# Head 4's root ahead of a pool operand, statistics two k steps sooner at four entries, and the first four low parts on VectorE

## What is computed

```python
h = rms_norm(x, g[0])                 # x0, x2: entries of the two mixers
m = parallel_conv_mla(h, ...)         # or conformer_conv
x = x + rms_norm(m, g[1])
h = rms_norm(x, g[2])                 # x1, x3: entries of the two MLPs
x = x + rms_norm(squared_relu_mlp(h, mlp_w1[i], mlp_w2[i]), g[3])
...
n1 = _rmsnorm(h, norm1_w)             # x4: entry of the second block
q, k, v, fg, u = jnp.split(n1 @ w_in, [...], axis=-1)
q = _rmsnorm(q.reshape(B, L, N_HEADS, HEAD_DIM), q_norm_w)
k = _rmsnorm(k.reshape(B, L, N_HEADS, HEAD_DIM), k_norm_w)
pooled = [_trailing_mean_minus_self(u[group g], w) for g, w in enumerate((2, 4, 8, 16))]
```

## Time and profile before

| | us |
|---|---|
| three runs | 1783.16, 1784.21, 1779.24; median 1783.16 |
| the profiled execution, its own time | 1780.72 |
| its span, first to last instruction | 1778.9 |
| TensorE busy | 1742.8, 98% |
| GpSimd busy | 886.8, 50% |
| VectorE busy | 793.2, 45% |
| ScalarE busy | 662.8, 37% |

### The profile page before, as it was taken

One profiled execution on the slowest core, in us unless ns is written; L12 is line 12 of the kernel. 1 busy time (PEld: TensorE's weight loads), 2 busy tenths in 40 slices (PEclk: granted clock), 3 DMA queues, 4 the chain that ended last, 5 costly groups with the idle time before them and its releaser, 6 DMA issues.

```text
span 1778.9 us, 22989 instructions
## 1 busy us (share of the span) xinstructions
PE 1742.8 (98%) x8243; PEld 1448.7 (81%) x8243; DVE 793.2 (45%) x1221; ACT 662.8 (37%) x1039; POOL 886.8 (50%) x477
## 2 busy tenths in 40 slices
PE   8999999999999999999999999999899999999999
PEld 6887887888888877878788888889878888888887
DVE  7458654301331479956430132147757244444200
ACT  6338543312222446554321232145357332222221
POOL 5457545444444469755544444445345644444442
PEclk9999999999999999999999999999999999999999
DMA  5532123233333213122333333322210333323332
GB/s 179 130 105 60 36 71 103 91 102 95 95 97 100 76 48 107 59 86 92 106 95 95 96 100 99 95 71 72 86 49 10 98 95 94 94 95 97 104 106 71
DMA packets 46074, 158.45 MB, mean 89 GB/s; under 512 B 5745, under 2 KB 6001, under 8 KB 46001
## 3 DMA queue, kind: packets, MB, share of 16 engines
q1 hardware_dynamic: 46000, 157.45, 28.5%
HBM read 153.10 MB, written 2.10 MB: 87 GB/s over the span
## 4 chain that ended last, share of the span: by engine, by line
PE 88%; DVE 6%; ACT 3%; issue 2%; POOL 1%; DMA 1%; SPq 0%; DVEq 0%; POOLq 0%; ACTq 0%
PE PS L1830 26%; PE PS L1832 25%; PE PS L1831 25%; PE PS L1899 2%; DVE PS L1218 1%; PE PS L1935 1%; PE PS L1930 1%; PE PS L1931 1%; PE PS L2091 1%; DMA raw<-weights 1%; DVE PS L1210 1%; PE PS L1840 0%; DVE XLR L1218 0%; ACT wh L727 0%; PE PS L2114 0%
## 5 line engine op out<-in xcount | busy, mean ns | idle before, releaser
L548 POOL TENSOR_TENSOR wl<-raw,wh 128x1024 fp32r<-128x1024 f32 x220 | 533.0, 2424 | 632.1 <-ACT wh L741 198.3
L1831 PE MATMUL PS<-XLR,wh 128*128 128x512 f32 x1216 | 474.4, 390 | 0.0
L1830 PE MATMUL PS<-XHR,wh 128*128 128x512 f32 x888 | 349.0, 393 | 9.3 <-POOL wl L617 6.0
L1832 PE MATMUL PS<-XHR,wl 128*128 128x512 f32 x888 | 346.8, 391 | 0.0
L1831 PEld LDWEIGHTS PS<-XLR,wh 128*128 128x128 f32 x1216 | 229.2, 188 | 47.3
L1830 PE MATMUL PS<-HH,wh 128*128 128x512 f32 x688 | 267.6, 389 | 0.0
L1831 PE MATMUL PS<-HL,wh 128*128 128x512 f32 x688 | 267.6, 389 | 0.0
L1832 PE MATMUL PS<-HH,wl 128*128 128x512 f32 x688 | 267.6, 389 | 0.0
L727 ACT ACTIVATE wh<-raw 128x1024 fp32r<-128x1024 f32 x123 | 128.6, 1055 | 240.0 <-PE PS L1832 196.6
L1830 PEld LDWEIGHTS PS<-XHR,wh 128*128 128x128 f32 x888 | 167.6, 189 | 45.1 <-POOL wl L617 6.4
L1832 PEld LDWEIGHTS PS<-XHR,wl 128*128 128x128 f32 x888 | 167.4, 189 | 35.1
(11 more groups left out here) (343 smaller groups left out, 2577.9 us busy)
## 6 DMA issues: line engine op xcount, KB each, us to landing
raw<-weights SPq DMA_DIRECT2D x287, 512.0 KB, 3.5
X<-x_t SPq DMA_DIRECT2D x8, 256.0 KB, 6.8
out_t<-X SPq DMA_DIRECT2D x8, 256.0 KB, 4.6
KH<-rope_h SPq DMA_DIRECT2D x4, 128.0 KB, 4.6
KL<-rope_l SPq DMA_DIRECT2D x4, 128.0 KB, 5.4
QH<-XHR SPq DMA_DIRECT2D x16, 32.0 KB, 2.0
QL<-XLR SPq DMA_DIRECT2D x16, 32.0 KB, 2.0
pos_i<-positions SPq DMA_DIRECT2D x1, 256.0 KB, 8.3
```

The lines of the kernel that those rows point to most:

```text
L548: pool.tensor_tensor(wl[:, j], raw[:, j], wh[:, j].bitcast(F32), ALU.subtract).then_inc(w_lo, 1)
L1830: pe.matmul(out, wa, xa, start=start, stop=False)
L1831: pe.matmul(out, wa, xb, start=False, stop=False)
L1832: return pe.matmul(out, wb, xa, start=False, stop=stop)
```

## The change

It has three parts. VectorE makes `wl` of blocks 0 to 3, one after each even x tile, and GpSimd waits for all four before its first block (4). In `enter_residual` the statistic stands at k = 3 in place of 5 and the spread at 5 in place of 7, at x1, x2, x3 and x4. On ScalarE `head_root(4)` stands directly behind `head_square(4)`, ahead of `pool_operand(3)` and `hi(n0 + 13)`.

```diff
-            lo_range(0, 5)
+            pool.wait_ge(w_lo, RING)
+            lo_range(RING, 5)
             zero_rows((KH, KL), 5, 0)
...
             head_square(4)
+            head_root(4)
             pool_operand(3)
             hi(n0 + 13)
-            head_root(4)
             head_round(4)
             head_square(5)
...
             for k in range(KT):
                 v.wait_ge(xh, k + 1)
                 stt(XL[:, k], X[:, k], ENTRY_GAIN["x0"](k), f(XH[:, k]), ALU.mult, ALU.subtract).then_inc(xl, 1)
+                if k % 2 == 0:
+                    v.wait_ge(w_hi, k // 2 + 1)
+                    tt(wl[:, k // 2], raw[:, k // 2], f(wh[:, k // 2]), ALU.subtract).then_inc(w_lo, 1)
...
-                tile(n0 + 3, last, {5: lambda: stat(entry), 7: lambda: spread(entry)},
+                tile(n0 + 3, last, {3: lambda: stat(entry), 5: lambda: spread(entry)},
                      order=range(ahead, KT), begun=True)
```

## The result

The changed kernel took 1766.18 us, median of 5 runs (1765.94 to 1770.06), against 1780.31 for the kernel before, median of 5 (1779.24 to 1784.21). The ratio is 0.9919, with a 95% interval from 0.9908 to 0.993: 14.1 us less. The profiled execution took 1765.98 us, 14.7 less than that of before. The forecast was 1772 us, in a range from 1766 to 1779, and the prediction's parts made 9.7.

A forecast was written before the change was run, and what follows sets the result against it. TensorE, busy 98% of the span, was taken as the bound. Parts 2.0 + 4.5 + 3.2 = 9.7 us gave 1771.0 from the profiled 1780.7 or 1773.5 from the median 1783.2; forecast 1772, range 1766 to 1779.

The forecast's parts named there:

- Part 1: Start: `wl` of four blocks on VectorE lets low parts of x come sooner; 2.0 us, between -0.8 and 2.3.
- Both terms: Start: TensorE goes on 0.9 us sooner after the fourth low part of x; two later waits going give 1.1.
- The two waits: Behind the start: TensorE's waits for `rcol` (0.3) and the latents' `ssq` (0.8) both go, 1.1 us.
- The loss of 1.7 by clock: Start: one more 3.5 us stretch at half clock would cost 1.7 us, making the low bound -0.8.
- Part 2: x1 to x4: statistics two k steps sooner; x1 and x3 2.7 together, x2 1.4, x4 0.4, sum 4.5 us.
- the wait named: x2: TensorE's wait of 5.97 us, until 670.64, becomes 1.36 shorter, down to 4.6.
- Rival (d): x entries: the statistics do nothing, as TensorE meets the block's `wl` instead of the bank; about 1777, chance 0.06.
- Part 3: Head 4: root sooner, so the wait ahead of its spread shrinks by 2.8 to 3.8; 3.2 us taken.
- the sentence on the clock behind the spread: Head 4: a shorter wait may leave the clock up from 1262.50 to 1266.50, saving 1.7; only in the high bound, 5.5.
- Rival (a): Head 4: its wait moves on to head 5, part 3 gives 1.5 or less; about 1778, chance 0.13.
- Rival (b): Head 4 and x2: no low-clock stretch after head 4, a shorter one at x2; 13 us, about 1768, chance 0.14.
- Rival (c): Start: clock stays at 1.2 GHz through the first four tiles; loss 21.8 less 9.7, time 1795, chance 0.02.

The follow-up runs named there:

- the filled start: Kernel before, with 8 matmuls that compute nothing needed in TensorE's start wait of 2.36 us for the second low part of x: 1780.71 against 1781.3, ratio 0.9996.
- the last experiment: Changed kernel with spread at k = 4 and filling matmuls in the layer norm's pairs, ahead of its spread and in head 4's last wait: 1768.48, ratio 0.9919.
- The filled wait: Kernel before, with 12 matmuls that compute nothing needed in TensorE's 3.8 us wait ahead of head 4's spread: 1775.95 against 1780.36, ratio 0.9977.
- GpSimd's load: Changed kernel with four GpSimd subtractions of a `wl`'s size, which nothing reads, put back at the start: 1772.57, ratio 0.9959.

## Why the prediction was wrong, step by step

**Part 1, 2.0 forecast, 3.1 measured.** The mechanism and the durations were right (`wl` on VectorE 1.22 against 1.26, low parts 0.74 against 0.74). Both terms were too small, by 0.6 and 0.4. TensorE went on at 12.69, not at 13.0, and the rest of the serial list was sooner too: 1.49 at the statistic of x0 where 0.9 stood. The two waits gave 1.46 where 1.1 stood. The loss of 1.7 by clock, the low bound, concerns a stretch that costs nothing in the kernel before (the filled start) and comes and goes; it does cost where TensorE has work through it, 2.2 us in the last experiment. The Trainium skill, "TensorE: Matmul & The Clock Gate", What's actually happening, says that the moment of a change is not tied to the kernel's start. The traces agree for the start and attention: two profiles of one kernel differ there.

**Part 2, 4.5 forecast, 4.4 measured.** x1 1.29 and x3 1.34 for 1.36 each, x2 1.37 for 1.4, x4 0.39 for 0.4. At x2 the size was right but not the wait named, so that the size came out is in part luck: the wait of 5.97 became 5.79 and not 4.6, and most of the rest was a wait of 0.92 for ScalarE's `wh` ahead of it, which I had not listed and which is gone. Rival (d) fell.

**Part 3, 3.2 forecast, 7.1 measured: the step that failed.** The wait shrank by 2.95, within the 2.8 to 3.8 given and for the reason given: `meta_x` was held up behind `pool_l`, 1.17 us for 0.21. The Trainium skill, "GPSIMD Engine Reference", Key points, made no exception for small copies, and the trace agrees with that. What failed is the sentence on the clock behind the spread, worth 1.7 "where VectorE isn't the one to wait for". I left it out of the sum and allowed it once. It was worth 4.1. The stretch that I had priced at 1.7 gave 2.15, and a second one behind head 5, which I had not counted, 1.97. VectorE was waiting for TensorE's products, so the low clock lay on the path twice, in TensorE's own list and in VectorE's, where small instructions slipped behind GpSimd. The filled wait gives the same 4.1 as the shortened one, so this is clock and not wait; only the second stretch's tie to the wait stays open. Rival (a) fell. Rival (b) was the right one in kind for head 4, with too small a price; the stretch at x2, its other half, did not get shorter.

**Outside the parts.** Attention gave 1.54 in the profile. That is not the change's: the stretch there is absent from the second profile of the kernel before too. Between x2 and x3 1.30 were lost, by the layer norm's longer stretch, which differs between two profiles of the kernel before as well (774 to 778 and 773.5 to 779.5). That the two nearly cancel, and so that the parts come close to the whole, is luck. 9.7 + 1.1 (part 1) - 0.1 (part 2) + 3.9 (part 3) + 1.5 - 1.3 = 14.8. The forecast of 1772 lay 1 us above the sum from the profiled execution, since it allowed for a median of 1783.2; with two more runs the median of the kernel before was 1780.31.

**Rival (c)** fell. Its condition, low clock while TensorE has work at the start, was seen in the last experiment and cost 2.2, a tenth of its price, as the clock was back by 18 us. Under GpSimd's load it cost 1.5.

What stays open: what decides whether a low stretch of the start, the layer norm or attention appears, and for how long. Runs of one kernel differ by 4 to 5 us, about as much as such stretches cost. The mean granted clock of each run points the same way: of the changed kernel's ten runs the five from 1765.9 to 1766.2 us have 0.996, the five from 1767.1 to 1770.1 have 0.994. By an estimate from these shares, 0.002 of 1764 us is 3.5 us of clock lost, or some 7 us more at half clock. Where in those longer runs the stretches lay, no profile shows.

## What to carry to other kernels

A long wait of TensorE is worth its own length and then the low clock behind it, if the engines that follow wait for TensorE's products there; count every low stretch behind it, and what slips behind another engine's long instructions meanwhile. A low stretch that ends inside a wait is worth nothing. That other engines are busy throughout is no proof that it is worth nothing. To price it, fill the wait with spare matmuls: here that held the clock and left the wait's end where it was. Fill one wait at a time, and read the gain from marks right behind it, or one filling's loss hides another's gain.

## What the runs showed of the hardware

- Tiny VectorE instructions are held up by GpSimd like large ones: `meta_x` of 16x128 took 1.17 for 0.21, `K2L` of 128x16 took 2.31 for 0.24, about the rest of the GpSimd instruction that ran.
- A low stretch has very different prices: 0 at the start before 13.9, where it lay in a wait; 2.2 behind the conformer's wait; 1.3 to 1.45 for the shorter against the longer in the layer norm; 2.15 and 1.97 behind heads 4 and 5; 1.5 in attention; 2.2 at the start when TensorE had work.
- Four GpSimd subtractions at the start, whose result nobody reads, cost 6.4 us of 1766 (5.5 in the profiled executions).
